# All eight heads in turns of four tiles, a first quarter loaded in halves, and early sums inside the last tile

## The reference

```python
h = rms_norm(x, norm1)
z = h @ w_in                                     # 2048 x 5120
u, q, f, i, g = split(z, [1024, 2048, 3072, 4096])
pool_out = pool_mix(u, cache, ...)               # trailing means over 2, 4, 8, 16 tokens, per-group linear map
forget = lb + (1 - lb) * sigmoid(f)
S_t = diag(forget_t) S_{t-1} + (1 - forget_t)^T i_t ;  o_t = silu(q_t) S_t      # 8 heads, 128 x 128 state
o = rms_norm(o, per head) * hg_norm * silu(g)
x = x + concat(pool_out, o) @ w_o                # 2048 x 2048
h2 = rms_norm(x, norm2)
x = x + (silu(h2 @ w_gate) * (h2 @ w_up)) @ w_down      # hidden width 5632
y = rms_norm(x, norm_f)
```

## Time and profile before

| | us |
|---|---|
| median of 3 runs | 1423.34 (1422.92 to 1425.15) |
| profiled execution | 1423.23 |
| its span, first to last instruction | 1421.50 |
| TensorE busy | 1400.9 (99%) |
| VectorE busy | 775.3 (55%) |
| ScalarE busy | 573.8 (40%) |
| GpSimd busy | 214.5 (15%) |
| share of the chain that ended last on TensorE | 96% |

### The profile page before, as it was taken

One profiled execution on the slowest core, in us unless ns is written; L12 is line 12 of the kernel. 1 busy time (PEld: TensorE's weight loads), 2 busy tenths in 40 slices (PEclk: granted clock), 3 DMA queues, 4 the chain that ended last, 5 costly groups with the idle time before them and its releaser, 6 DMA issues.

```text
span 1421.5 us, 27766 instructions
## 1 busy us (share of the span) xinstructions
PE 1400.9 (99%) x10256; PEld 1384.9 (97%) x10256; DVE 775.3 (55%) x1206; ACT 573.8 (40%) x926; POOL 214.5 (15%) x329
## 2 busy tenths in 40 slices
PE   8999999999999999999999999999999999999996
PEld 7999999999999999999999999999999999999996
DVE  5668888878555544444444444444444444444443
ACT  6545555656333433333333333333333333333343
POOL 0355555553122100000000000000000000000131
PEclk9999999999999999999999999999999999999998
DMA  8556655556555555545655555565554565555453
GB/s 253 152 135 166 170 158 149 154 148 167 148 148 148 148 148 148 148 130 144 174 143 148 148 138 143 148 167 157 144 157 120 151 175 151 151 148 138 122 142 114
DMA packets 408228, 214.65 MB, mean 151 GB/s; under 512 B 4205, under 2 KB 405821, under 8 KB 408124
## 3 DMA queue, kind: packets, MB, share of 16 engines
q1 hardware_dynamic: 388775, 202.01, 52.2%
q10 hardware_dynamic: 19413, 12.10, 3.0%
HBM read 206.20 MB, written 7.89 MB: 151 GB/s over the span
## 4 chain that ended last, share of the span: by engine, by line
PE 96%; DVE 1%; DMA 1%; ACT 0%; issue 0%; ACTq 0%; DVEq 0%
PE bank L427 30%; PE bank L429 30%; PE bank L428 30%; DMA xt<-in_x_sample 1%; PE bank L544 1%; DVE w_lo L1200 0%; PE bank L777 0%; PE bank L503 0%; PE bank L504 0%; PE bank L671 0%; PE bank L505 0%; PE bank L643 0%; PE bank L596 0%; PE bank L472 0%; PE bank L652 0%
## 5 line engine op out<-in xcount | busy, mean ns | idle before, releaser
L427 PE MATMUL bank<-a_hi,w_hi 128*128 128x320 f32 x2016 | 626.5, 311 | 0.0
L429 PE MATMUL bank<-a_hi,w_lo 128*128 128x320 f32 x2016 | 623.0, 309 | 0.0
L428 PE MATMUL bank<-a_lo,w_hi 128*128 128x320 f32 x2016 | 622.9, 309 | 0.0
L1200 DVE TENSOR_TENSOR w_lo<-w_raw,w_hi 128x1024 fp32r<-128x1024 f32 (+1 forms) x412 | 455.5, 1146 | 137.1 <-ACT w_hi L821 136.3
L821 ACT ACTIVATE w_hi<-w_raw 128x1024 fp32r<-128x1024 f32 (+1 forms) x412 | 383.6, 968 | 158.8 <-PE bank L429 142.4
L427 PEld LDWEIGHTS bank<-a_hi,w_hi 128*128 128x128 f32 x2016 | 378.6, 188 | 1.5 <-issue 0.6
L428 PEld LDWEIGHTS bank<-a_lo,w_hi 128*128 128x128 f32 x2016 | 378.6, 188 | 0.7
L429 PEld LDWEIGHTS bank<-a_hi,w_lo 128*128 128x128 f32 x2016 | 378.5, 188 | 0.0
L427 PE MATMUL bank<-h_hi,w_hi 128*128 128x320 f32 x704 | 218.5, 310 | 0.0
L429 PE MATMUL bank<-h_hi,w_lo 128*128 128x320 f32 x704 | 217.4, 309 | 0.0
L428 PE MATMUL bank<-h_lo,w_hi 128*128 128x320 f32 x704 | 217.3, 309 | 0.0
(11 more groups left out here) (252 smaller groups left out, 1193.7 us busy)
## 6 DMA issues: line engine op xcount, KB each, us to landing
w_raw<-in_w_gate SPq DMA_DIRECT2D x44, 1024.0 KB, 5.6
w_raw<-in_w_up SPq DMA_DIRECT2D x44, 1024.0 KB, 5.6
w_raw<-in_w_down SPq DMA_DIRECT2D x64, 704.0 KB, 4.8
w_raw<-in_w_in SPq DMA_DIRECT2D x38, 1024.0 KB, 5.8
w_raw<-in_w_o SPq DMA_DIRECT2D x16, 1024.0 KB, 6.1
s<-in_state_hgrn ACTq DMA_DIRECT2D x8, 512.0 KB, 4.3
out<-sn ACTq DMA_DIRECT2D x8, 512.0 KB, 5.4
xt<-in_x_prompt SPq DMA_DIRECT2D x6, 256.0 KB, 8.5
```

What stands on the lines that cost most here:

```text
L427: pe.matmul(out, whi[:, par_, cols], r_hi, start=(k == 0), stop=False)
L428: pe.matmul(out, whi[:, par_, cols], r_lo, start=False, stop=False)
L429: last = pe.matmul(out, wlo[:, par_, cols], r_hi, start=False, stop=(k == last_k))
L1200: dve.tensor_tensor(wlo[:, par_, cols], raw[:, par_, cols], whi[:, par_, cols].bitcast(F32), SUB)\
```

## The change

Three things are changed.

*The heads.* EARLY is gone. All eight heads have turns of four units in one loop, on every engine, with loads in that order; the three-unit turns, `onb` and `keep_out` fall away. Head 7's recurrence is put into units O0 and O0+1. TensorE runs tiles 0 to 7 of unit O0, the state, tiles 8 to 14, the output, tiles 0 to 12 of O0+1, the turning back, tiles 13 and 14; then it waits for head 7's gate, and runs tile 15 of O0 and tile 15 of O0+1. ScalarE and VectorE split unit O0+2 around the gate.

*The start.* The first quarter of x and weights is loaded in two halves, of tiles 0 to 1 and 2 to 3, so that there are five chunks; the second half's weights come through ACT's queue, as the second quarter's did. TensorE's transposes stand behind the matmuls of a tile, not ahead. One of four filler products is left out. The chunks of weights are split behind tiles 0, 2, 5 and 9.

*The end.* The early sums stand after tile 7 of the last unit, which has 11 tiles. VectorE scales y in five pieces, with the samples last and in halves. Waits of ScalarE for earlier stores are placed ahead of the loop and in the last block.

```diff
-EARLY = 5
-L0 = H0 + 4 * EARLY
-G0 = L0 + 3 * (HEADS - EARLY)
-O0 = G0 + HEADS - EARLY
+O0 = H0 + 4 * HEADS
...
+        CHUNKS = ((0, 2), (2, 4), (4, 8), (8, 12), (12, 16))
+        BEHIND = (0, 2, 5, 9)
...
-        Y_DVE = ((0, slice(0, 512)), (0, slice(512, 1024)), (2, slice(0, D)), (1, slice(0, 1024)))
+        Y_DVE = ((0, slice(0, 512)), (0, slice(512, 1024)), (1, slice(0, 1024)), (2, slice(0, 1024)), (2, slice(1024, D)))
...
-            for quarter in range(4):
-                load_x(sp, quarter, 0)
-                if quarter >= 2:
-                    load_x(sp, quarter, 1)
-                if quarter != 1:
-                    first_weights(sp, quarter)
+            for chunk in range(5):
+                load_x(sp, chunk, 0)
+                if chunk >= 3:
+                    load_x(sp, chunk, 1)
+                if chunk != 1:
+                    first_weights(sp, chunk)
...
-            keep_busy(4)
+            keep_busy(3)
...
-            for k in range(AHEAD):
+            for k in range(2):
                 x_transposes(k)
 
             for k in range(KD):
-                if k + AHEAD < KD:
-                    x_transposes(k + AHEAD)
...
+                for ahead in ((2, 3) if k == 0 else (k + AHEAD,)):
+                    if ahead < KD:
+                        x_transposes(ahead)
...
+            def part_of(j, k0, k1, used=0):
...
+            own = KD - 1
+            pe.wait_ge(unit_read, O0 - 1)
+            pe.wait_ge(mp_lo_s, HEADS)
+            pe.wait_ge(gm_hi, HEADS - 1)
+            pe.wait_ge(gm_lo, HEADS - 1)
+            part_of(0, 0, 8, used=1)
+            rec_state(HEADS - 1)
+            part_of(0, 8, own)
+            rec_out(HEADS - 1)
+            pe.wait_ge(unit_read, O0)
+            part_of(1, 0, 13)
+            rec_back(HEADS - 1)
+            part_of(1, 13, own)
+            pe.wait_ge(gm_hi, HEADS)
+            pe.wait_ge(gm_lo, HEADS)
+            part_of(0, own, KD, used=1)
+            part_of(1, own, KD, used=2)
...
-            for quarter in range(4):
-                if quarter < 2:
-                    load_x(act, quarter, 1)
-                if quarter == 1:
+            for chunk in range(5):
+                if chunk < 3:
+                    load_x(act, chunk, 1)
+                load_x(act, chunk, 2)
+                if chunk == 1:
                     first_weights(act, 1)
-                load_x(act, quarter, 2)
...
             rec_tokens(HEADS - 1)
+            silu_g(HEADS - 1, O0 - 1)
             decayed(HEADS - 1)
-            silu_g(EARLY, G0)
-            split_hi(G0 + 2, 1)
-            gate_split(EARLY)
+            split_hi(O0 + 1, 1)
             rec_squares(HEADS - 1)
             rec_stores(HEADS - 1)
...
+            rec_scale(HEADS - 1)
+            act.wait_ge(raw_loaded[0], 8 * (O0 + 2) - 16)
+            hi_piece(O0 + 2, 0, 0, HALF[0])
+            gate_split(HEADS - 1)
+            hi_piece(O0 + 2, 0, 1, HALF[1])
```

More of the change, by code:

```diff
@@ L210, in hybrid_kernel @@
                              "cache_loaded", "s0_loaded"))
-        x_loaded = [[sem(f"x_loaded{quarter}{i}") for i in range(3)] for quarter in range(4)]
-        w_first = [sem(f"w_first{quarter}") for quarter in range(4)]
+        x_loaded = [[sem(f"x_loaded{chunk}{i}") for i in range(3)] for chunk in range(5)]
+        w_first = [sem(f"w_first{chunk}") for chunk in range(5)]
         first_hi, first_lo, w2_loaded, w3_loaded, x_pad = (
@@ L378, in _ @@
                     load(2 * i + k, k, win_v, (0, KD), (2 * i + k) * P)
-            with sp.Fori(0, EARLY) as h:
+            with sp.Fori(0, HEADS) as h:
                 for j, part in enumerate((2, 1, 3, 4)):
                     load(H0 + 4 * h + j, j % 2, win_v, (0, KD), part * PW + h * P)
-            for h in range(EARLY, HEADS):
-                for j, part in enumerate((2, 1, 3)):
-                    n = L0 + 3 * (h - EARLY) + j
-                    load(n, n % 2, win_v, (0, KD), part * PW + h * P)
-            for g in range(EARLY, HEADS):
-                n = G0 + g - EARLY
-                load(n, n % 2, win_v, (0, KD), 4 * PW + g * P)
             with sp.Fori(0, KD // 2) as i:
@@ L655, in rec_out @@
             def rec_out(r):
[L656 to L659 removed]
+                after(pe, gated, r)
                 pe.wait_ge(s1_ready, r + 1)
@@ L795, in column_means, with early_means @@
                         last.then_inc(signal, 1)
-                    pe.wait_ge(x2_acc, KD - 1)
-                    for bk in (TV, OT):
-                        pe.matmul(bk[:, 2:3], acc[:, N - P:N], meanc[:, 0:1], start=True, stop=True)
-                    column_means(TV, acc, y_early)
+                    def early_means():
+                        pe.wait_ge(x2_acc, KD - 1)
+                        for bk in (TV, OT):
+                            pe.matmul(bk[:, 2:3], acc[:, N - P:N], meanc[:, 0:1], start=True, stop=True)
+                        column_means(TV, acc, y_early)
+                    unit(nd + KD - 2, 0, h_rhs, HALF_D, between=(None, y_tiles(KD - 3, 1)))
+                    unit(nd + KD - 1, 1, h_rhs, HALF_D, between=(early_means, y_tiles(KD - 2, 0)))
                     pe.wait_ge(last_sq, 1)
@@ L838, in square @@
                 rows, at = (P if i < 2 else NS), 2 * i + half
-                for quarter in range(2 * half, 2 * half + 2):
-                    act.wait_ge(x_loaded[quarter][i], 16)
+                for chunk in ((0, 1, 2), (3, 4))[half]:
+                    act.wait_ge(x_loaded[chunk][i], 16)
                 after(act, ss_ready, squares[0])
@@ new lines, in _, with mixed @@
+            gate_lo(HEADS - 1)
+            lo_piece(O0 + 2, 0, 1, HALF[1])
+            def mixed(j, k):
+                done(O0 + j)
+                dve.tensor_tensor(x1[:, j, :], x1[:, j, :], zb[k][:, 0:N], ADD).then_inc(unit_read, 1)
+                dve.wait_ge(h2_hi, j + 1)
+                dve.scalar_tensor_tensor(out=a_lo[:, j, :], in0=x1[:, j, :], scalar=pcol("norm2", j),
+                                         in1=a_hi[:, j, :].bitcast(F32), op0=MUL, op1=SUB).then_inc(h2_lo, 1)
+            mixed(0, 0)
@@ L1777, in _ @@
             rec_sample(0)
-            with pool.Fori(1, EARLY) as h:
-                keys(h)
-                key_copies(h)
-                rec_sample(h)
-            for h in range(EARLY, HEADS):
+            with pool.Fori(1, HEADS) as h:
                 keys(h)
```

205 lines of the change are left out of this document (66 added, 139 removed).

## The result

The changed kernel takes 1426.1 us (median of 17 runs, 1424.22 to 1428.70), the kernel before 1423.35 (17 runs, 1421.62 to 1425.95). The ratio is 1.0020, 95% interval 1.0014 to 1.0027: slower by 0.2%, or 2.8 us (2.0 to 3.8). The forecast was 1421.3, with a range of 1419.0 to 1423.9; the time lies outside it, on the other side of the kernel before.

A forecast was written before the change was run, and what follows sets the result against it. TensorE, busy nearly throughout, was taken as the bound. On the profiled 1423.23 us, -2.9 - 5.1 + 4.1 + 0.7 + 1.2 + 1.0 - 0.9 = -1.9 gave 1421.3 us, range 1419.0 to 1423.9.

The forecast's parts named there:

- A: At the start: loading half the bytes first and moving transposes behind matmuls saves 2.9 us (1.2 to 3.8).
- By bytes (648 KB instead of 1160 on that queue) I put the new one at 10.5: At the start: the second small weight piece on ACT's queue lands at 10.5, against 13.9 for the old piece.
- a rival at 0.12: At the start: nothing gained if the small weight piece lands late; 1424.2 us, slower by 0.9; chance 0.12.
- What comes last there in the changed order: At the start, tile 6: its high part waits for the third later weight piece; tile 6 at 19.9 instead of 22.80.
- What tile 6 gains the rest keeps: At the start: TensorE runs without a gap after tile 6, so its gain, 22.80 to 19.9, carries through.
- B: Old heads 5 to 7: four-tile turns remove the idling of their three-tile turns, saving 5.1 us.
- D: Loop ends of the heads: the loop closes six times, not three, at 0.22 us more each; 0.7 us added.
- C: New end of head 7: two TensorE waits, of 1.6 and 2.5 us, add 4.1 us (1.0 to 5.0).
- E: Behind head 7's end: the two waits bring 3.3 us at half clock, adding 1.2 us (0 to 1.6).
- The rival that the clock stays: Behind head 7's end: the clock stays at 2.4 GHz since the stream before is dense; 1420.1 us; chance 0.28.
- F: Early sums in the middle of the last tile: ten instructions lose their free cover, adding 1.0 us (0.8 to 1.2).
- G: Last stores: samples in two halves of 4 KB rows and last save 0.9 us (0 to 1.8).

The follow-up runs named there:

- e13: The changed kernel with two of ScalarE's ten load issues (samples of the last two pieces) moved behind its first high part: 1426.51 us.
- e11: The changed kernel with transposes standing four tiles ahead instead of three at the start: 1423.4 us in one run.
- e2: The kernel before with only the heads changed (four-tile turns for all eight, new end of head 7): 1426.1 us, ratio 1.0018.
- e12: The changed kernel with three filler matmuls, one in the first wait at head 7's end and two in the second: 1424.32 us in one run.
- e1: The kernel before with only the changed kernel's start (five loads, new order of transposes and conversions): 1424.97 us, ratio 1.0003.
- e5: The changed kernel with VectorE's gate ahead of the first low piece and the first bank's read ahead of the second: 1422.32 us.
- e7: The changed kernel with the second small weight piece converted behind tile 1 instead of tile 0: 1426.93 us.
- e14: The changed kernel, halves kept, with two load issues behind the second high part, two weight conversions later and transposes four tiles ahead: 1424.5 us.
- e3: The kernel before with only the early sums moved into the middle of the last tile: 1424.53 us, ratio 1.0006.
- e4: The kernel before with only the order and sizes of VectorE's last scalings and their stores changed: 1423.11 us, ratio 0.9995.

## Why the prediction was wrong, step by step

**A, the start: the largest miss, -2.9 forecast, +0.4 (-0.9 to +1.9) measured.** Four steps of it failed.

- "By bytes (648 KB instead of 1160 on that queue) I put the new one at 10.5": the second small weight piece landed at 13.06 in the profiled execution, and between 11.4 and 14.9 in ten traces with loads in halves. I had priced that case as a rival at 0.12, "decides from a landing after about 13", tile 1 at 16; it came at 15.44. The mechanism was named and its chance was far too low.
- "What comes last there in the changed order" (at tile 6): not the third piece of weights. TensorE's own stream did: tile 1 at 15.44, then one tile after the other at half clock, then 1.21 a tile. The piece I had landing at 16.8 landed at 18.6 (issued at 6.2, 12.4 to landing), and was not waited for.
- The clock. I let it stay at full speed at the start, and priced a fall only into the bound. TensorE idles 2.92 us ahead of tile 0, and 0.50 is granted from 11.8 to 18.6. ScalarE's load issues, which I also had in the bound only, are why tile 0 comes no sooner: the first halves are there at 6.1, and ScalarE is not (e13). They are not the whole of the fall: in e13 tile 0 is at 10.18, tile 1 still waits, and 0.50 is granted from 15.9 to 19.3.
- "What tile 6 gains the rest keeps": it loses 0.67 again at tiles 9 to 15, as each transposition now stands a tile later (e11).

The Trainium skill (DMA: Bandwidth & Descriptors, "Rules for kernel authors") wants at least 1 MiB in a transfer, and by that I had let A shrink to -1.2. No trace here settles whether smaller pieces cost rate. The last piece of the first weights lands at 21.6 instead of 19.4, but it was also issued 2.1 us later (8.26 for 6.14) and took 13.3 in both. From 2 to 19 us the queues move 273 GB/s in the changed kernel's trace and 294 in that of before; with halves it is 285 in e11, with whole quarters 279 in e2.

**B, the old last heads: right.** No idle time from 260 to 350 us. **D, loop ends:** not seen alone. With no fall (e12, 448.43, against e1 with the same start, 448.64) B, C and D together are -0.2, forecast -0.3; C is 4.2 in the rows, so B and D together are -4.4, forecast -4.4. How the 4.4 is split between them is not shown.

**C, the end of head 7: right.** 1.61 and 2.56 us where 1.6 and 2.5 were forecast, with six matmuls between, ended by the two instructions named. e5 shows that VectorE's order is the cause.

**E, the clock behind it: the mechanism right, the size wrong.** 1.2 forecast (0 to 1.6). All six kernels with both full waits fell (changed, e2, e7, e11, e13, e14), four for 3.4 us and two for 6.8; none fell with shorter ones. A fall costs 1.5 where it lasts 3.4 us, and 2.0 or 2.8 where it lasts 6.8. I had taken the one length that the start of before showed; e3 and e4, whose start is the same, have 6.8 us there. One trace gave a length, not a bound. The rival that the clock stays (0.28) is out. The Trainium skill (TensorE: Matmul & The Clock Gate, "Why this matters for your kernels") lets the clock fall after longer idle gaps only; the measurement decides, and here it falls after 1.6 us, six matmuls and 2.6 us.

**F, the early sums: right**, +1.04 for +1.0. **G, the stores: mis-sized**, -0.9 forecast, -0.2 in the mean of the rows, -0.7 (-2.0 to +0.6) in the runs. The stretch at 236 GB/s goes with the 8 KB rows, but with rows of 4 KB the last two us of full queues still run at 283 and 291 (e4), where I had taken 373 throughout. Why, the runs don't show.

The sum: forecast -1.9, measured +2.8. A is 3.3 of the difference, E up to 1.6, G 0.2 to 0.7. The parts run alone add up to 0.4 + 2.6 + 0.9 - 0.7 = 3.2. The range failed with A: its upper end took tile 6 at 21.6 as the worst, when the rows of before already had a piece on that queue landing 11 us after its issue.

Open: why the small piece lands at 11.4 in one execution and at 14.9 in another, and why the tail of the stores is slow at its end.

## What to carry to other kernels

On an in-order engine, look at what stands ahead of the one instruction that the bottleneck waits for: moving the gate ahead of a weight piece gave back 5.2 us between the marks, and moving a conversion and the transposes behind the tiles that don't need them gave 2.7, with the same loads in nearly the same order. Loading less first bought nothing here, since the engine that converts it was not free and the next piece came late; count an engine's load issues as work. Where two idle stretches like these (1.6 and 2.6 us) come close together, price a fall of the clock at what several traces show, not one.
